# Reordering the high-half and low-half matmuls over two k tiles in a TensorE-bound two-layer trunk

## What is computed

```python
def reference(x, ...):
    h = x                                    # (1, 256, 2048)
    for layer in range(2):
        hn = rms_norm(h, mix_norm[layer])
        if layer % 2 == 0:
            mix = swa_sink_attention(hn, w_qkv, b_qkv, sinks, w_o, b_o)
        else:
            mix = rglru_block(hn, w_in, ..., w_out, b_out)
        h = h + mix
        hn = rms_norm(h, mlp_norm[layer])
        h = h + jnp.square(jax.nn.relu(hn @ w_up[layer])) @ w_down[layer]
    return rms_norm(h, final_norm)
```

## Time and profile before

| | |
|---|---|
| median of 3 runs | 2025.28 us (2025.14 to 2028.07) |
| the profiled execution | 2027.66 us, of it 2025.7 us from the first instruction to the last |
| TensorE matmul busy | 1999.9 us (99%), 11604 matmuls |
| weight loads busy | 1747.6 us (86%) |
| VectorE busy | 1358.7 us (67%) |
| ScalarE busy | 1057.6 us (52%) |
| mean granted TensorE clock | 0.995 |
| DMA | 368 MB, 182 GB/s |

### The profile page before, as it was taken

One profiled execution on the slowest core, in us unless ns is written; L12 is line 12 of the kernel. 1 busy time (PEld: TensorE's weight loads), 2 busy tenths in 40 slices (PEclk: granted clock), 3 DMA queues, 4 the chain that ended last, 5 costly groups with the idle time before them and its releaser, 6 DMA issues.

```text
span 2025.7 us, 34215 instructions
## 1 busy us (share of the span) xinstructions
PE 1999.9 (99%) x11604; PEld 1747.6 (86%) x11604; DVE 1358.7 (67%) x1560; ACT 1057.6 (52%) x1438; POOL 8.7 (0%) x12
## 2 busy tenths in 40 slices
PE   9999999999999999999999999999999999999997
PEld 8888888888888888888888888888888888888886
DVE  7777676656655665667688887666566556656665
ACT  7555454444444444445588885544444444444453
POOL 1000000000000000000000000000000000000000
PEclk9999999999999999999999999999999999999998
DMA  8433556556565655565655555565566556555652
GB/s 276 141 104 115 195 169 207 190 184 193 180 197 177 199 190 188 180 195 175 209 178 185 180 166 183 176 207 187 186 186 187 195 178 197 187 188 178 202 171 90
DMA packets 365879, 368.12 MB, mean 182 GB/s; under 512 B 11536, under 2 KB 363920, under 8 KB 365712
## 3 DMA queue, kind: packets, MB, share of 16 engines
q1 hardware_dynamic: 365552, 365.53, 57.0%
q0 software_dynamic: 288, 2.10, 0.3%
HBM read 365.48 MB, written 2.10 MB: 181 GB/s over the span
## 4 chain that ended last, share of the span: by engine, by line
PE 90%; DVE 5%; ACT 2%; issue 2%; DMA 0%; DVEq 0%; ACTq 0%; SPq 0%
PE ps L1256 58%; PE ps L1259 29%; DVE w_lo L766 2%; PE aux L1276 1%; PE aux L1277 1%; PE aux L1278 1%; DVE xc L1145 0%; ACT L616 0%; DVE u L780 0%; PE aux L1292 0%; DVE v L1102 0%; PE aux L1329 0%; DMA h<-x_l_dram 0%; DVE h L1241 0%; ACT w_hi L343 0%
## 5 line engine op out<-in xcount | busy, mean ns | idle before, releaser
L766 DVE TENSOR_TENSOR w_lo<-w_raw,w_hi 128x1024 fp32r<-128x1024 f32 x678 | 816.7, 1223 | 336.3 <-ACT w_hi L343 335.2
L343 ACT ACTIVATE w_hi<-w_raw 128x1024 fp32r<-128x1024 f32 x678 | 701.7, 1054 | 434.7 <-PE ps L1259 432.1
L1256 PE MATMUL ps<-xn,w_hi 128*128 128x512 f32 x2880 | 908.4, 397 | 3.7 <-DVE xn L834 2.3
L1256 PE MATMUL ps<-mid,w_hi 128*128 128x512 f32 x2544 | 800.8, 396 | 1.9 <-DVE mid L903 1.5
L1259 PEld LDWEIGHTS ps<-xn,w_lo 128*128 128x128 f32 x2880 | 541.8, 188 | 128.3
L1259 PEld LDWEIGHTS ps<-mid,w_lo 128*128 128x128 f32 x2544 | 478.7, 188 | 113.2
L1259 PE MATMUL ps<-xn,w_lo 128*128 128x256 f32 x2880 | 566.7, 278 | 0.0
L1259 PE MATMUL ps<-mid,w_lo 128*128 128x256 f32 x2544 | 500.5, 278 | 0.0
L1256 PEld LDWEIGHTS ps<-xn,w_hi 128*128 128x128 f32 x2880 | 439.4, 189 | 5.8 <-issue 5.1
L1256 PEld LDWEIGHTS ps<-mid,w_hi 128*128 128x128 f32 x2544 | 388.0, 189 | 2.6 <-issue 2.6
L780 DVE TENSOR_TENSOR u<-ps,half 128x512 f32<-128x512 f32 x170 | 117.4, 691 | 182.9 <-ACT half L356 160.9
(11 more groups left out here) (154 smaller groups left out, 808.2 us busy)
## 6 DMA issues: line engine op xcount, KB each, us to landing
w_raw<-mlp_w_up_dram SPq DMA_DIRECT2D x256, 512.0 KB, 3.8
w_raw<-mlp_w_down_dram SPq DMA_DIRECT2D x256, 512.0 KB, 3.4
w_raw<-b_w_in_dram SPq DMA_DIRECT2D x64, 512.0 KB, 4.9
w_raw<-a_w_qkv_dram SPq DMA_DIRECT2D x40, 512.0 KB, 5.2
w_raw<-a_w_o_dram SPq DMA_DIRECT2D x32, 512.0 KB, 3.7
w_raw<-b_w_out_dram SPq DMA_DIRECT2D x32, 512.0 KB, 4.4
h<-x_l_dram SPq DMA_DIRECT2D x4, 512.0 KB, 8.5
gate_raw<-b_gate_a_w_dram SPq DMA_DIRECT2D x8, 256.0 KB, 2.8
```

What stands on the lines that cost most here:

```text
L343: nc.scalar.activation(w_hi[:, s, :, :], w_raw[:, slot, :, :], ACT.Copy).then_inc(hi_ready, 1)
L766: nc.vector.tensor_tensor(w_lo[:, s, :, :], w_raw[:, slot, :, :], w_hi[:, s, :, :].bitcast(F32), ALU.subtract).then_inc(lo_ready, 1)
L1256: nc.tensor.matmul(ps[:, 2 * half_i + b, :], hi[:, k, b * PART:(b + 1) * PART], operand[:, :, kt, :], start=kt == 0, stop=False)
```

## The change

Inside a chunk the matmuls of two k tiles are taken together. Before, each k tile had two long matmuls (block 0, block 1) and then two short ones. Now two k tiles have four long ones (blocks 0, 1, 0, 1) and then four short ones in the same order. Number, shapes, operands and targets of the matmuls stay as they are, and so do the waits ahead of the chunk and the signal on its last matmul. The start flag stays on the first long matmul of each bank.

```diff
-                for k in range(CH_KT):
+                def long(k, b):
                     kt = s * CH_KT + k
-                    for b in range(2):
-                        nc.tensor.matmul(ps[:, 2 * half_i + b, :], hi[:, k, b * PART:(b + 1) * PART],
-                                         operand[:, :, kt, :], start=kt == 0, stop=False)
-                    for b in range(2):
-                        last = nc.tensor.matmul(ps[:, 2 * half_i + b, TOK:2 * TOK], lo[:, k, b * PART:(b + 1) * PART],
-                                                operand[:, 0, kt, :], start=False, stop=kt == KT - 1)
+                    nc.tensor.matmul(ps[:, 2 * half_i + b, :], hi[:, k, b * PART:(b + 1) * PART],
+                                     operand[:, :, kt, :], start=kt == 0, stop=False)
+
+                def short(k, b):
+                    kt = s * CH_KT + k
+                    return nc.tensor.matmul(ps[:, 2 * half_i + b, TOK:2 * TOK], lo[:, k, b * PART:(b + 1) * PART],
+                                            operand[:, 0, kt, :], start=False, stop=kt == KT - 1)
+
+                for k in range(0, CH_KT, 2):
+                    for at in (k, k + 1):
+                        for b in range(2):
+                            long(at, b)
+                    for at in (k, k + 1):
+                        for b in range(2):
+                            last = short(at, b)
                 last.then_inc(wts_used, 1)
```

## The result

The changed kernel takes 2038.1 us (median of 4 runs, 2036.6 to 2039.75) beside 2026.67 us before (4 runs, 2025.14 to 2028.07). The ratio is **1.0058, interval 1.0042 to 1.0074**: slower by 0.6%. Forecast was 2021.8 us, a small gain. The span of the profiled execution went from 2025.7 to 2037.8 us, by 12.1.

The account below looks back on a forecast made before the run. TensorE's matmul rate was taken as the bound. Fewer width changes gave -3.8 us, 0.3 us lost to waits, so -3.5 from 2025.28 made 2021.8 us; 8-in-10 range 2008 to 2044 us.

Parts of the forecast that it names:

- What bounds: Whole kernel: TensorE's matmul rate sets the time, matmuls busy 1999.9 of 2025.7 us; the other engines wait for it.
- The 28 ns of a pair that are not columns: Chunks: a long and a short matmul take 348.0 ns together, their columns 320.0; 28.0 ns remain.
- A constant per matmul: Chunks: each matmul costs its columns and some 14 ns, long 227, short 121, so order matters little; chance 0.55.
- only where the start is stamped: Single trace rows in chunks: the 233 and 115 ns of long and short reflect start stamping, not real costs.
- The step that failed: Groups of eight matmuls: each change of width costs 1.4 ns; two fewer save 2.8 ns a group, 3.8 us in all.
- The total held where the details moved: Two late chunks with weights in other buffers: 2.79 and 2.78 us beside 2.784, taken as support that order matters little.
- The slow rival: Runs of four short matmuls: short ones fall to the weight loads' 120 ns, long keep 233; 2052 or 2038 us; chance 0.24.
- The fast rival: Runs of four long matmuls: long ones fall to 227 ns, short stay at 115; 2001 or 2013 us; chance 0.19.
- 0 for PSUM, buffers and banks: Chunk ends and bank alternation: `wts_used` comes when it came, banks still alternate, returning sooner to a bank costs nothing.

Follow-up runs that it names:

- pace: Changed kernel plus added runs of 48 matmuls of one width and chunks in four orders: 120.0 ns a step at 256 columns, 226.7 at 512.
- pace_2: Changed kernel plus added matmuls of 512 and 256 columns in runs of n and n: rounds of four cost 16.7 ns above uniform pace.
- order_8: Kernel with all eight long matmuls of a chunk, then all eight short ones: 2030.54 us, ratio 1.0017 to the kernel before.
- order_16: Kernel with chunks alternately eight long then eight short, and eight short then eight long: 2025.23 us, ratio 0.9984 to the kernel before.
- order_2_by_block: Two long, two short as before, but the two are two k tiles of one block: 2026.86 us, ratio 0.9995 to the kernel before.
- order_4_swapped: Four long, four short like the change, but short ones go block 1, 0, 1, 0: 2039.32 us, ratio 1.0064 to the kernel before.

## Why the prediction was wrong

- **What bounds.** Right. TensorE's rate was the whole story; waits, clock, and the other engines' programs stayed, and the span moved with TensorE's busy time.
- **The 28 ns of a pair that are not columns.** Right, and 26.7 of them are a constant of 13.3 ns per matmul (pace). A constant per matmul, with the division 233 and 115 "only where the start is stamped", held for uniform runs alone.
- **The step that failed** is "The 0.7 ns x 8 = 5.6 ns a group, if they belong to the four changes of width, are 1.4 ns each. Two changes fewer save 2.8 ns". The 0.7 ns are real, 0.8 by the start times: a chunk of before stands 2787 - 2773 = 14 ns above the uniform pace, 7 a group. They do come from alternating widths (pace_2). But they are not a price per change. A round of two and two costs 3.3 ns, one of four and four 16.7. A group had two rounds of 3.3 and now has one of 16.7, so **+10 ns in place of -2.8**, 1360 x 10 = 13.6 us in place of -3.8, of which 11.4 us (medians) and 12.1 us (spans) were measured. Nothing in the trace of before could give the price of a round of another length; I had one length and a uniform run, and drew a line through them.
- **"The total held where the details moved".** The two late chunks (2.79 and 2.78 us) were the evidence that order doesn't matter. They have the same order as the others; I read a test of the entry as one of the order.
- **The slow rival.** Its outcome is nearest: "about half, 2038 us", 10 ns a group. That is luck: the 10 ns are 13.3 more for the four short ones and 3.3 less for the four long ones, which it left at 233. The short ones do go towards 120, as it says. Its cause, that the loads' pace holds them there, fell: a load-bound stream steps at 112 ns and not at 120 (pace), longer runs of short ones cost less and not more (8 and 8, 16 and 16), and 512 and 384 columns cost 20 ns a round with no matmul near a load's length (pace_2).
- **The fast rival**, long ones near 227 once they have no short neighbours, is real but needs runs longer than four: it is what order_8 and order_16 get. The short ones don't stay at 115 then.
- **Nothing moved elsewhere:** 0 for PSUM, buffers and banks was right (order_2_by_block, order_4_swapped).

Open: what inside TensorE makes the first five matmuls after a shorter width late, by 7, 9, 2, 6 and 4 ns on average. The steps depend on the sequence of widths and on what stood ahead of it, not on buffers or banks. Every matmul here has a weight load, so no run shows whether the loads as such, apart from their pace, have a part in it. That the steps come from some fixed beat between two parts of the engine is a guess that no run here tested.

## What to carry to other kernels

When two kinds of matmul of different width share a stream, the pattern of widths has a price that is neither per matmul nor per change: here 3.3 ns above uniform pace for a round of 2 + 2, 16.7 for 4 + 4, 20 from 6 + 6 on, so either stay short or make the runs as long as the buffers allow. By the table of pace_2, runs of 2 and of 12 are equal in ns a pair, and all between are worse. A price that the trace shows at one run length only must not be carried to another; some hundred added matmuls into an unused bank measure it in one run. And where a chunk is periodic, read the single steps: the same median over a whole window can hide two rhythms.

## What was not expected of the hardware

- Each matmul with a weight load of its own costs 13.3 ns above its columns (120.0 ns at 256, 226.7 at 512). The Trainium skill's page "TensorE: Matmul & The Clock Gate" (Back-to-back issue gap) has 2.5 ns for the isolated gap of a matmul; here it is five times as much. No run here leaves the loads out, so that they are the reason is not shown.
- One and one has two steady rhythms, 346.7 and 353.3 ns a pair, each held for hundreds of microseconds, and runs of the kernel that uses it differ by 15 us (2034.22 to 2049.04).
- The clock fell in pace near the end of the run of 48 matmuls of 64 columns, and the run of 128 columns went at 213 ns a step. The windows of pace, over the one run and the other:

```profile
32.00:37.00 5.00, 5.00 (x47) 4.97 (x45) 3.58 (x3) 0.92 (x2) 0.00 (x0) 1.00 1.10 348
38.00:48.00 10.00, 10.00 (x49) 10.00 (x48) 0.00 (x0) 0.00 (x0) 0.00 (x0) 0.50 0.09 29
```

  The granted clock is 1.00 and then 0.50, the lower of its two levels, 1.2 GHz, though TensorE has no idle time in either window. Ahead of the fall, at 37.0 us, it had issued matmuls of 64 columns since 31.9 us, one every 112 ns. The clock stayed at 0.50 through the run of 128 columns and came back at 54.1 us, within the run of 192.
